# Another order of side work on VectorE, ScalarE and TensorE, and a value product written the other way round

## The reference, cut to what matters

```python
p_rw, q, c_kv, iq, ik, iw, gates = _split(rmsnorm(x) @ w_in, IN_SPLITS)
y_a = _rwkv7_time_mix(p_rw, ...) @ w_branch_rwkv     # 16 heads of 64, a recurrence over the tokens
y_b = _dsa_attention(q, c_kv, iq, ik, iw, ...) @ w_branch_dsa
h = x + (sigmoid(g_a) * y_a + sigmoid(g_b) * y_b) @ w_out

# inside _dsa_attention, for 16 heads and 128 queries at a time (top 64 keys by an index score):
pr = softmax(q k^T * SA_SCALE + bias, where allowed)
o = pr @ v                                            # 256 keys, 64 columns a head

# inside _rwkv7_time_mix, a step of the recurrence for one head, S is 64 x 64:
S = S * w_t + (S @ -kk_t) (kk_t * a_t)^T + v_t k_t^T ;  y_t = S @ r_t
# then a normalization of y over each head (mean and variance), times ln_x_w, plus ln_x_b,
# plus a bonus term, times a gate
```

## Time and profile before

| | |
|---|---|
| median of 3 runs | 3614.83 us (3608.24 to 3614.94) |
| the profiled execution | 3604.66 us, span 3602.5 us |
| TensorE, VectorE, ScalarE busy | 98%, 60%, 49% of the span |
| granted TensorE clock, mean | 0.994 |
| the stage that the change touches | 0 to about 820 us |

### The profile page before, as it was taken

How to read it: one execution, slowest core, us unless ns; L and a number is a source line. 1 busy time by engine, 2 the same in 40 slices (tenths; PEclk the granted TensorE clock), 3 DMA queues, 4 the chain that set the end, 5 groups by cost and what they waited for, 6 DMA issues and landing times. The chain is left out here.

```text
span 3602.5 us, 50879 instructions
## 1 busy us (share of the span) xinstructions
PE 3526.9 (98%) x20474; PEld 2996.6 (83%) x20474; DVE 2161.6 (60%) x2883; ACT 1753.3 (49%) x2613; POOL 342.3 (10%) x217
## 2 busy tenths in 40 slices
PE   8999999999999999999999999999999999999999
PEld 7777777778899999888899998887788887788777
DVE  4777555765577487555544465556777875565454
ACT  5553333333544686444444444444655654444753
POOL 0000000000089500000000000000122210000000
PEclk9999999999999999999999999999999999999999
DMA  6554333454545455555555665554534335455344
GB/s 227 180 191 156 119 127 131 169 211 175 199 176 187 169 181 177 211 186 188 189 207 186 221 246 221 188 188 174 192 135 144 132 138 195 169 195 189 119 141 164
DMA packets 111180, 638.55 MB, mean 177 GB/s; under 512 B 17738, under 2 KB 23658, under 8 KB 39192
## 3 DMA queue, kind: packets, MB, share of 16 engines
q1 hardware_dynamic: 106664, 622.98, 48.3%
q0 software_dynamic: 4336, 13.14, 1.1%
HBM read 611.10 MB, written 21.54 MB: 176 GB/s over the span
## 5 line engine op out<-in xcount | busy, mean ns | idle before, releaser
L222 DVE TENSOR_TENSOR lo_w<-ring,hi_w 128x1024 fp32r<-128x1024 f32 x500 | 612.3, 1225 | 970.6 <-ACT hi_w L216 962.0
L216 ACT CAST hi_w<-ring 128x1024 fp32r<-128x1024 f32 x540 | 569.0, 1054 | 948.5 <-DMA ring<-in_wstream 924.0
L224 DVE TENSOR_TENSOR lo_w<-ring,hi_w 128x1024 fp32r<-128x1024 f32 x500 | 612.2, 1224 | 0.0
L2033 PE MATMUL PS<-hi_x,lo_w 128*128 128x256 f32 x2048 | 580.1, 283 | 0.0
L2033 PE MATMUL PS<-hi_x,hi_w 128*128 128x256 f32 x2048 | 576.6, 282 | 3.2 <-POOL lo_w L224 3.2
L2033 PE MATMUL PS<-lo_x,hi_w 128*128 128x256 f32 x2048 | 571.4, 279 | 0.0
L217 ACT CAST hi_w<-ring 128x1024 fp32r<-128x1024 f32 x540 | 564.8, 1046 | 0.0
L2059 PE MATMUL PS<-hi_w,hi_g 128*128 128x512 f32 x1024 | 404.0, 395 | 1.4 <-issue 1.4
L2059 PE MATMUL PS<-lo_w,hi_g 128*128 128x512 f32 x1024 | 403.4, 394 | 0.0
L2059 PE MATMUL PS<-hi_w,lo_g 128*128 128x512 f32 x1024 | 403.2, 394 | 0.0
L2033 PEld LDWEIGHTS PS<-hi_x,hi_w 128*128 128x128 f32 x2048 | 389.0, 190 | 3.6 <-issue 1.9
(11 more groups left out here) (583 smaller groups left out, 5756.4 us busy)
## 6 DMA issues: line engine op xcount, KB each, us to landing
ring<-in_wstream SPq DMA_DIRECT2D x540, 1024.0 KB, 4.8
other_G<-staged SPq DMA_DIRECT2D x32, 256.0 KB, 6.0
hot<-other_G SPq DMA_DIRECT2D x8, 1024.0 KB, 6.9
gates_dram<-gst POOLq DMA_DIRECT2D x8, 512.0 KB, 4.8
x_dram<-x SPq DMA_DIRECT2D x2, 2048.0 KB, 11.9
x<-x_dram SPq DMA_DIRECT2D x2, 2048.0 KB, 9.7
prev<-RKV POOLq DMA_DIRECT2D x6, 508.0 KB, 5.4
x<-in_x SPq DMA_DIRECT2D x4, 512.0 KB, 7.0
```

Of the source, the lines that this page charges most:

```text
L216: a.copy(hi_w[s][:, 0:HALF], ring[s][:, 0:HALF]).then_inc(S(f"hi{s}"), 1)
L222: v.tensor_tensor(lo_w[s][:, 0:HALF], ring[s][:, 0:HALF], hi_w[s][:, 0:HALF].bitcast(F32), ALU.subtract)
L224: v.tensor_tensor(lo_w[s][:, HALF:UNIT], ring[s][:, HALF:UNIT], hi_w[s][:, HALF:UNIT].bitcast(F32), ALU.subtract)\
L2033: m = nc.tensor.matmul(PS[:, s, 0:T], wa[s][:, k * P:(k + 1) * P], xa[:, k, :], start=(k == 0 and p == 0), stop=(k == KC - 1 and p == 2))
```

## The change

1. The value product is written with the operands exchanged: the values are the stationary operand (128x64) and the transposed probabilities the moving one (128 columns); the two heads of a pair go to the two halves of PSUM's partitions, head by head in turn. `turn_o` and `turned_o` are gone; `out_o` copies straight to `oT`, reading the columns of each block in reversed order.
2. For units below 34, `pv` and `turn_p` stand in the middle of the unit, in front of its third quarter; ACT's `turned_p` stands behind `hi` and `exps`.
3. `spread` moves to the head of pass 44 + 12n, in front of that pass's `lo`. `fades` and DVE's `WU` copy follow `joined` directly, in front of `lo`.
4. Section 3: the three parts of `solve` come one and a quarter, one and a quarter, and half a unit earlier (76.0, 76.25 and 77.75 in passes and quarters), `off_block` a unit and a half later. `finish` is cut into `finish_sum` and `finish_gate`; those of section 2 move to pass 79. The second `center` and `finish` of section 3 are gone.
5. The four `turn_y` stand at (80, 0), (80, 1), (83, 3), (85, 1) as (unit, quarter), before at (79, 0), (79, 1), (79, 2), (85, 1). DVE's `turned_y` of blocks 0, 1 and 3 stand in front of `lo`.

```diff
-    TURN_U = WIN + 3
+    TURN_AT = ((WIN + 4, 0), (WIN + 4, 1), (WIN + 7, 3), (WIN + 9, 1))
+    mid_unit = lambda b: b < 33
...
                 if p == 8:
-                    t.wait_ge(S("oo"), 1)
-                for e in range(2):
-                    h = 2 * j + e
-                    for k in range(tt + 1):
-                        m = nc.tensor.matmul(PS[:, 6 + h // 8, (h % 8) * 64:(h % 8 + 1) * 64], pT[:, e * (tt + 1) + k, :],
-                                             vv[:, k, h * 64:(h + 1) * 64], start=(k == 0), stop=(k == tt))
+                    t.wait_ge(S("o_T"), 1)
+                for k in range(tt + 1):
+                    for e in range(2):
+                        h = 2 * j + e
+                        m = nc.tensor.matmul(PS[half(e), 6 + j // 4, (j % 4) * P:(j % 4 + 1) * P], vv[:, k, h * 64:(h + 1) * 64],
+                                             pT[:, e * (tt + 1) + k, :], start=(k == 0), stop=(k == tt))
...
                 if n == 0:
-                    t.wait_ge(S("oo"), 2)
+                    t.wait_ge(S("o_T"), 2)
...
-                if n == 3:                        # in first
-                    t.wait_ge(S("ya_lo"), 3)
+                if n == 3:                        # in second
+                    t.wait_ge(S("ya_lo"), 2)
+                if n == 2:                        # in turn_y
+                    t.wait_ge(S("RW_sb"), 4)
...
-                if b - 2 in PAIR:
+                if b - 2 in PAIR and not mid_unit(b):
                     pv(PAIR[b - 2])
-                if b - 1 in PAIR:
+                if b - 1 in PAIR and not mid_unit(b):
                     turn_p(PAIR[b - 1])
-                if b == 26:
-                    turn_o(0)
                 for g in range(4):
-                    if (u, g) == (35, 2):
-                        turn_o(1)
+                    if g == 2 and b - 2 in PAIR and mid_unit(b):
+                        pv(PAIR[b - 2])
+                    if g == 2 and b - 1 in PAIR and mid_unit(b):
+                        turn_p(PAIR[b - 1])
+                    if (u, g) in TURN_AT:
+                        turn_y(TURN_AT.index((u, g)))
...
-                a.copy(oo, PS[:, 6:8, :].rearrange("p b c -> p (b c)")).then_inc(S("oo"), 1)
+                a.copy(oT[:, :, tile(tt)], PS[:, 6:8, :].rearrange("p b (k c) -> p (b k) c", k=4)[:, :, ::-1]).then_inc(S("o_T"), 1)
...
                 for n in due(U, 0, 10.75):
                     joined(n)
-                if U == RB + 3 * RSTEP + 12.75:
+                    fades(n)
+                    copy4(n, WU, 4, "W_ps", "W_v")
+                if U == WIN:
+                    solve(3, 0)
+                if U == WIN + 3:
+                    finish_sum(2)
+                    gated(WIN + 3)
+                if U == WIN + 8:
                     center(3)
+                    turned_y(2)
                     gated(u)
-                    finish(3)
+                    finish_sum(3)
+                    finish_gate(3)
                 elif WIN + 5 <= u < OUT and (u - WIN) % 2:
                     gated(u)
-                if U == WIN + 3:
-                    gated(WIN + 3)
...
-                for n in due(U, 1, 10):
+                for n in due(U, 0, 8.75):
                     spread(n)
+                if U == WIN + 4:
+                    turned_y(0)
+                    turned_y(1)
+                if U == WIN + 9:
+                    turned_y(3)
                 if u + 3 < OUT + 5:
                     lo(u + 3)
+                if U == WIN + 3:
+                    finish_gate(2)
...
                     for n in due(U, g, 15.75):
-                        center(n)
+                        if n < 3:
+                            center(n)
                     for n in due(U, g, 16.25):
-                        finish(n)
-                    for n in due(U, g, 5.25):
+                        if n < 2:
+                            finish_sum(n)
+                            finish_gate(n)
+                    for n in late_due(U, g, 5.25, 6.75):
                         off_block(n)
...
-                        for n in late_due(U, g, 6 + k / 4, 6 + (0, .25, 1)[k]):
-                            solve(n, k)
+                        for n in due(U, g, 6 + k / 4):
+                            if n < 3:
+                                solve(n, k)
+                    if (U, g) == (WIN, 1):
+                        solve(3, 1)
+                    if (U, g) == (WIN + 1, 3):
+                        solve(3, 2)
```

More of the change, by code:

```diff
@@ L349, in build @@
     qr0 = at_(8192, "qr0", (P, NT, 512))
-    oo = qr0[:].rearrange("p t c -> p (t c)")
     pen = at_(12288, "pen", (P, NT, T))
@@ L718, in qk @@
                     t.wait_ge(S("q_T"), 1)
-                if j == 4 and tt == 0:
+                if p == 2:
                     t.wait_ge(S("q_T"), 2)
-                if p == 10:
-                    t.wait_ge(S("o_T"), 1)
                 if p:
@@ L744, in pv @@
                 if p == 8:
-                    t.wait_ge(S("oo"), 1)
-                for e in range(2):
-                    h = 2 * j + e
-                    for k in range(tt + 1):
-                        m = nc.tensor.matmul(PS[:, 6 + h // 8, (h % 8) * 64:(h % 8 + 1) * 64], pT[:, e * (tt + 1) + k, :],
-                                             vv[:, k, h * 64:(h + 1) * 64], start=(k == 0), stop=(k == tt))
-                m.then_inc(S("pv"), 1)
[L753 to L759, removed]
+                    t.wait_ge(S("o_T"), 1)
[4 more added lines that the diff above has]
+                                             pT[:, e * (tt + 1) + k, :], start=(k == 0), stop=(k == tt))
+                m.then_inc(S("pv"), 1)
             def turn_z():
@@ L993, in _ @@
                 for g in range(4):
-                    if (u, g) == (WIN + 9, 1):
-                        turn_y(3)
-                    if (u, g) == (35, 2):
-                        turn_o(1)
+                    if g == 2 and b - 2 in PAIR and mid_unit(b):
[4 more added lines that the diff above has]
+                        turn_y(TURN_AT.index((u, g)))
                     for c in range(NCH):
@@ L1024, in _ @@
                         reads(n)
-                    if u == TURN_U and g < 3:
-                        turn_y(g)
                     quarter(u, g)
@@ L1092, in out_o @@
                 a.wait_ge(S("pv"), 8 * tt + 8)
-                if tt:
-                    a.wait_ge(S("o_ps"), 1)
-                a.copy(oo, PS[:, 6:8, :].rearrange("p b c -> p (b c)")).then_inc(S("oo"), 1)
-            def turned_o(tt):
-                a.wait_ge(S("o_ps"), tt + 1)
-                a.copy(oT[:, :, tile(tt)], PS[:, 3:5, :].rearrange("p b (k c) -> p (b k) c", k=4)).then_inc(S("o_T"), 1)
+                a.copy(oT[:, :, tile(tt)], PS[:, 6:8, :].rearrange("p b (k c) -> p (b k) c", k=4)[:, :, ::-1]).then_inc(S("o_T"), 1)
             def state(n, c):
@@ L1225, in _ @@
                     a.drain().then_inc(S("q_T"), 1)
-                if u - 1 in PAIR:
+                if u - 1 in PAIR and not mid_unit(u):
                     turned_p(PAIR[u - 1])
[L1228 to L1231, removed]
+                if u == 34:
+                    out_o(1)
                 if u == 33:
@@ L1245, in _ @@
                     exps(PAIR[u])
+                if u - 1 in PAIR and mid_unit(u):
+                    turned_p(PAIR[u - 1])
+                if u == 25:
+                    out_o(0)
                 if u == 23:
@@ L1257, in _ @@
                 for g in range(4):
[L1258 to L1261, removed]
                     for n in due(U, g, 11.5):
@@ L1289, in _ @@
                         a.copy(rkv_of(n)[1], PS[:, 5, :]).then_inc(S("Y_sb"), 1)
+                    if (U, g) in TURN_AT:
+                        turned_y(TURN_AT.index((U, g)))
                     for n in late_due(U, g, 16, 13):
@@ L1292, in _ @@
                         a.activation(s8[:, 6, :], s8[:, 5, :], ACT.Sqrt, bias=GN_EPS, scale=1.0 / HD).then_inc(S("gn_std"), 1)
-                    if U == TURN_U and g:
-                        turned_y(g - 1)
             a.wait_ge(S("gate_out"), 128)
@@ L1584, in joined @@
                 v.drain().then_inc(S("two_v"), 1)
-                fades(n)
             def copy4(n, dst, b, ready, done):
@@ L1619, in center, with finish_sum @@
                 v.drain().then_inc(S("gn_var"), 1)
-            def finish(n):
+            def finish_sum(n):
                 r_, y_, v_ = rkv_of(n)
@@ L1632, in finish, with finish_gate @@
                 v.drain()
+            def finish_gate(n):
+                r_, y_, v_ = rkv_of(n)
                 tt_(y_, y_, lwlb[:, 1, :], ALU.add)
@@ L1740, in _ @@
                 for g in range(4):
-                    if (U, g) == (WIN + 9, 2):
-                        turned_y(3)
                     for n in due(U, g, -3):
@@ L1769, in _ @@
                     for k in range(3):
-                        for n in late_due(U, g, 6 + k / 4, 6 + (0, .25, 1)[k]):
```

(7 more changed lines are left out.)

## The result

The changed kernel takes 3584.0 us (median of 4 runs, 3579.33 to 3586.63), the kernel before 3614.89 (4 runs): a ratio of 0.9911, 95% interval 0.9895 to 0.9926. The gain is 30.9 us, where 16.2 were forecast; 3584.0 lies 2 us under the lower end of the range. Its profiled execution took 3584.97 us, span 3582.8, mean granted clock 0.992.

The account below looks back on a forecast made before the run. TensorE, busy 98% of the span, bounds the kernel; 34.0 us of its waits were the direct ceiling. Terms 10.5 + 2.4 - 3.0 - 4.5 + 10.8 = 16.2 us gave 3614.83 - 16.2 = 3598.6 us, range 3586 to 3611.

Parts of the forecast that it names:

- half-clock terms: TensorE at 1.2 GHz behind waits: 1.6 us gained in attention; 1.5, 1.6, 1.6, 1 lost in sections 0 to 3.
- attention: Value product, `turn_o` removal and `turn_p` in mid-unit: 10.5 us gained, 4 to 14, including 1.6 of half clock.
- section 0: `second` 1.5 us forward, `WU` copy gives 2.4, half clock behind `second` costs 1.5: 2.4 us gained, 0 to 4.
- section 1: `spread` waits for the copy back, `second` 2.6 us later, `WU` copy gives 1.2, half clock costs 1.6: 3.0 lost.
- section 2: Same as in the section before, with the copy back landing 1.5 us later: 4.5 us lost.
- section 3: Earlier substitution, `WU` copy, `turned_y` ahead of `lo`, no second `center` and `finish`: 10.8 us gained, 4 to 14.
- exchanged product: Attention's value product with operands exchanged: 3.0 us gained, 4.2 lost, net 1.2 lost, apart from 3.5 for `turn_o`.
- pairing: Value product's two heads run side by side in alternating halves: 3.0 us gained over 16 pairs.
- the middle of the unit: Placing the exchanged product there adds two changes of shape for 14 pairs, some 0.3 us each: 4.2 us lost.
- The slower rival: Attention: `scale_p` waits for the later `turn_p`, delaying DVE and the next `qk`; 25 us lost, 3624; chance 0.06.

Follow-up runs that it names:

- b_again: The kernel before, unchanged, traced and timed again: 3616.98 us over 12 runs, ratio 0.9999; the traced execution's span was 3616.3 us.
- b_third: The kernel before, unchanged, a third trace: 3613.07 us, one run.
- mid_only: The kernel before with only `pv` and `turn_p` moved in front of the third quarter, product and `turn_o` as they were: 3602.75 us, 0.9959.
- pv_only: The kernel before with only the exchanged value product, `turn_o` and its copies gone, `pv` and `turn_p` at the unit's head: 3612.30 us, 0.9985.
- spread_first: The kernel before with only `spread` moved to the head of pass 44 + 12n, in front of `lo`: 3624.76 us, 1.0022.
- copies_first: The kernel before with only `fades` and DVE's half of the `WU` copy directly behind `joined`, in front of `lo`: 3603.85 us, 0.9963.
- no_second_norm: The kernel before with only the second `center` and `finish` of section 3 removed: 3615.90 us, 0.9991.
- late_spread: The changed kernel with `spread` behind `lo` of its pass instead of in front: 3576.28 us, 0.9892 to the kernel before.
- attn_only: The kernel before with only parts 1 and 2 of the change, the attention's two edits: 3601.02 us, 0.9963.
- one1_first: The changed kernel with `spread` behind its `lo` and DVE's `one1` copy in front of the next pass's `lo`: 3573.18 us, 0.9882 to the kernel before.

## Why the prediction was wrong

The first column is what the prediction gives a part with its half-clock terms left out, the others the difference of that stretch of units at full rate against the three traces of after, first for `b_again` and `b_third`, then for the trace that the prediction was made from:

```
                           forecast   b_again, b_third   first trace
attention   (units 15-36)     8.9       9.9 to 10.2      11.8 to 11.9
section 0   (units 36-48)     3.9       2.3 to 2.7        2.7 to 3.0
section 1   (units 48-60)    -1.4      -1.6 to -1.3      -1.2 to -0.9
section 2   (units 60-72)    -2.9      -2.3 to -1.2      -2.3 to -1.3
section 3   (units 72-94)    11.8      10.5 to 11.1      10.9 to 11.5
sum                          20.3      19.7 to 21.0      22.7 to 23.6
```

The 11.8 of section 3 still holds a half clock: the prediction gives `first` of before 3.5 us "with half clock", and its 16 matmuls take 2.05 at full rate. Without it the section is 10.4, the sum 18.9, and the half-clock terms of the prediction are together a loss of 2.7 us, not 4.1.

**The order was read rightly in the main**, 19 to 20 us where 20 to 24 came. The exchanged product was not: the prediction has pairing give 3.0 us and the middle of the unit cost 4.2, 1.2 lost on balance. In the changed kernel a unit like 22 went from 6.80 to 6.91 us and one like 31 from 7.68 to 7.57, which comes out even. The cost is not where it was put: the product moved as it was costs nothing (`mid_only`), the exchanged one at the head of the unit gives 6.93 and 7.57 us (`pv_only`), so the exchange brings its change of shape with it, at the head or in the middle. `turn_p` keeps 0.43 us at unit 17 (0.6 forecast) and 0.37 at unit 34 (1.17). The slower rival, the loop through DVE, did not come: no new wait stands in these units. In section 1 `spread` waits 3.92 us, as worked out (459.3 - 455.4 = 3.9), and `second` 4.05 us (4 forecast). Section 2:

```profile
563.08 1.23 DVE L1554 TENSOR_TENSOR TT<-TC,blockm 128x1024 f32<-128x1024 f32 x1 [4.38 <-DMA TC<-T_dram]
```

4.38 us, and 4.53 in front of `second`, where 5.4 and 5.5 were forecast: the copy back came 1 us sooner. In section 3, DVE and POOL:

```profile
683.62 1.23 DVE L1554 TENSOR_TENSOR TT<-TC,blockm 128x1024 f32<-128x1024 f32 x1 [0.19 <-issue]
```

```profile
671.60 1.09 POOL L1320 DMA_DIRECT2D T_dram<-Xs  x2 [3.25 <-DVEq L1547]
```

The substitution ends at 671.6; TensorE is by then 7.5 us ahead of the trace of before, so that is 679.1 in the prediction's times (679 forecast), and `spread` follows with no wait for the copy, at 691.1 (691.6). `second` waits 2.78 us there.

**The step that failed is the half-clock terms** (+1.6 in the attention, -1.6, -1.6, -1.5 and -1 in the sections), with the line that carries them to the median: "That execution lay 10.2 us under the median of the runs shown; against the median the forecast is 3614.83 - 16.2". They say that the change costs clock, some 3 to 4 us; against the usual executions of before it gives 8 to 13 back. They were read off one trace, in which there was little half rate behind waits to lose, and the line takes the 10.2 us as an offset of every run. They were in the main clock: 0.994 in that execution, 0.988 in the usual one. Against that one execution the terms have the right sign in two traces of three: half-rate time went from 37.5 to 47.8, 41.0 and 37.5 us. It does stand behind `second` in section 1, where the prediction put it, 3.4 us in the profiled execution and 6.8 in the other two:

```profile
454.53 3.65 PE L856 MATMUL PS<-one,x 128*128 128x128 f32 x16 [4.05 <-issue]
```

(1.95 us for the same 16 matmuls at full rate.) One reading behind these terms was wrong too: the prediction sets the length of wait that has half rate behind it between 2.8 and 3.6 us, but its own trace has 3.4 us at 0.50 from 716.8 us on, behind the 2.71 us wait in front of `states` of section 3. Span against span the gain is 3602.5 - 3582.8 = 19.7 us, 3.5 over the forecast. But the changed kernel's execution was one of its usual ones (3584.97 us, median 3584.0) and that of before was not. Against usual executions of before the clock term has the other sign: 0.0042 more, some 11 us gained by the line, not 4 lost. The prediction had the warning in its hands: the three times beside the profile, 3608 to 3615, and a traced 3604.66 under all of them. It should have asked what made that one faster before it used its clock.

Where the higher clock comes from can be told in part. TensorE's waits in the stage (one trace; of before, `b_again`) beside the mean clock of all timed runs:

```
                 waits us  clock          waits us  clock
spread_first       40.8    0.9872   mid_only     29.3   0.9903
before             34.9    0.9877   copies_first 27.7   0.9898
pv_only            35.2    0.9885   after        18.4   0.9919
no_second_norm     32.7    0.9875   late_spread  15.0   0.9932
attn_only          28.1    0.9890   one1_first    8.3   0.9928
```

Fewer waits go with a higher clock, though not one by one (`attn_only` and `mid_only`, `late_spread` and `one1_first` stand the other way round). The table by places above says where: the waits of `turn_p` and `states` took with them the half-rate time behind them, 37.5 us of it with unit 35's in `b_again` and 34.1 in `b_third`, where the three traces of after have 10.2, 0 and 0. The waits of `second` brought 13.7 to 20.5 in place of the 13.7 behind `first`. Why the clock falls behind a wait, these runs do not tell.

**What stays open.** Which wait makes the clock fall, and when, is not settled: the 2.61 us wait above was followed by half rate in one execution and not in another. Nor is it why the `chain` runs partly at half rate without a wait, or how the 30.9 us divide between order and clock to better than some 5 us.

## What to carry to other kernels

Look at how the profiled execution lies among the timed runs and compare its clock with theirs; where it is apart, forecast at equal clock and price the clock by a line through time and clock of many runs. A wait can cost more than its length: count what the clock loses behind it, and take that from more than one trace. When a late operand is moved forward in an engine's list, ask what it meets there: here it waited 3.9 us with work queued behind it, and setting it behind one piece that was ready gave 8 us in the medians, 2 to 3 of them by the order. An edit that only moves a wait (`spread_first`) can cost alone and still pay beside the edit that empties its new place.

## What the runs showed of the hardware

The half-rate time of one program differs from execution to execution by a factor of two: 37.5, 78.5 and 68.3 us in this stage, with the same waits but for one of 0.9 us, and with DVE and ACT busy for the same time to 0.2 us. Its places mostly recur: it stands behind waits of 1.2 to 5.3 us, and where TensorE waits for nothing. At 392.8 us of `b_again` TensorE was busy all of 6.8 us at 0.50, in the row above, with its last wait over 20 us back, and all six traces of the two kernels have 3.4 to 10.2 us at 0.50 in each of units 47, 59 and 71. The Trainium skill, "TensorE: Matmul & The Clock Gate", section "What's actually happening", says of the stretch at a kernel's start that how many matmuls run cold varies from one run to another, and that one should not fit to one count. These traces show a variation of that kind in the middle of a kernel; here it is worth up to 15 us in a stage of 700.
